# Two attentions whose probabilities are divided before they are turned, with the values stationary and two heads in the column halves

## What is computed

```python
# attention A (one block of 256 keys, so plain causal attention), dh = 64
y_a = softmax(causal(q_a @ k_a.T / 8)) @ v_a
# attention B, q and k of 96 features (64 + 32 rotated), values of 64
y_b = softmax(causal(q_b @ k_b.T / sqrt(96))) @ v_b
merged = sigmoid(gate_a) * (y_a @ w_branch_a) + sigmoid(gate_b) * (y_b @ w_branch_b)
x = x + merged @ w_out
```

## Time and profile before

| | |
|---|---|
| time, 3 runs | 1725.09 us median (1724.26 to 1725.42) |
| the profiled execution | 1723.3 us, span 1721.6 us |
| TensorE busy | 1689.4 us, 98% of the span |
| DVE, ACT, POOL busy | 939.0, 986.0 and 1025.6 us |
| mean granted TensorE clock | 0.997 of full |
| the loop of 16 units | about 86.9 to 141.6 us of the span |
| 84 to 142 us | TensorE busy 56.90 of 58.00 us, DVE 20.51, ACT 36.09, POOL 27.85 |

### The profile page before, as it was taken

One profiled execution on the slowest core, in us unless ns is written; L12 is line 12 of the kernel. 1 busy time (PEld: TensorE's weight loads), 2 busy tenths in 40 slices (PEclk: granted clock), 3 DMA queues, 4 the chain that ended last, 5 costly groups with the idle time before them and its releaser, 6 DMA issues.

```text
span 1721.6 us, 30763 instructions
## 1 busy us (share of the span) xinstructions
PE 1689.4 (98%) x9832; PEld 1457.8 (85%) x9832; DVE 939.0 (55%) x1895; ACT 986.0 (57%) x1894; POOL 1025.6 (60%) x549
## 2 busy tenths in 40 slices
PE   9999999999999999999999989999999999899998
PEld 7887998888888888888888888988999877799997
DVE  6233378897999995555555557752111277421112
ACT  5565654445988885544455466526454565554544
POOL 4846768877777772000000078528888886578886
PEclk9999999999999999999999999999999999999999
DMA  6534545555444446565555645115555554355553
GB/s 224 177 99 133 203 157 183 186 176 187 160 160 160 160 160 197 193 195 193 190 193 193 222 142 159 62 50 177 184 190 186 171 181 138 92 184 184 193 184 121
DMA packets 83074, 288.19 MB, mean 167 GB/s; under 512 B 9264, under 2 KB 9264, under 8 KB 82480
## 3 DMA queue, kind: packets, MB, share of 16 engines
q1 hardware_dynamic: 82560, 286.10, 50.8%
q10 hardware_dynamic: 432, 1.05, 0.2%
HBM read 285.01 MB, written 2.10 MB: 167 GB/s over the span
## 4 chain that ended last, share of the span: by engine, by line
PE 91%; DVE 3%; ACT 3%; POOL 2%; issue 1%; DMA 0%; DVEq 0%; ACTq 0%; POOLq 0%
PE col L943 14%; PE acc L640 14%; PE acc L641 14%; PE acc L642 14%; PE col L945 7%; PE col L677 5%; PE col L679 5%; PE col L678 5%; POOL w_lo L2012 1%; PE mb L958 1%; PE mb L959 1%; PE acc L1155 1%; PE mb L712 1%; ACT hT L1463 1%; ACT w_hi L1439 1%
## 5 line engine op out<-in xcount | busy, mean ns | idle before, releaser
L2012 POOL TENSOR_TENSOR w_lo<-w_raw,w_hi 128x1024 fp32r<-128x1024 f32 (+1 forms) x403 | 954.9, 2387 | 295.9 <-ACT w_hi L1439 295.0
L1439 ACT ACTIVATE w_hi<-w_raw 128x1024 fp32r<-128x1024 f32 (+1 forms) x539 | 564.1, 1050 | 334.9 <-PE acc L642 278.0
L943 PE MATMUL col<-hT,w_hi 128*128 128x512 f32 x1024 | 368.9, 403 | 0.6 <-DVE acc L2527 0.6
L945 PE MATMUL col<-hT,w_lo 128*128 128x256 f32 x1024 | 286.5, 280 | 0.0
L943 PEld LDWEIGHTS col<-hT,w_hi 128*128 128x128 f32 x1024 | 192.3, 188 | 45.8 <-issue 1.5
L640 PE MATMUL acc<-w_hi,W_hi 128*128 128x512 f32 x512 | 199.3, 389 | 0.3 <-DVE act_e L2654 0.3
L642 PE MATMUL acc<-w_hi,W_lo 128*128 128x512 f32 x512 | 199.2, 389 | 0.0
L641 PE MATMUL acc<-w_lo,W_hi 128*128 128x512 f32 x512 | 199.2, 389 | 0.0
L945 PEld LDWEIGHTS col<-hT,w_lo 128*128 128x128 f32 x1024 | 193.5, 189 | 0.0
L2054 POOL TENSOR_SCALAR_AFFINE_SELECT WST<-WST 128x512 f32<-128x512 f32 x1 | 0.9, 940 | 319.5 <-DMA WST<-in_gmlp_w 319.5
L2938 DVE CAST H_hi<-mb 128x256 fp32r<-128x256 f32 x64 | 27.2, 425 | 289.3 <-ACT mb L1865 289.3
(11 more groups left out here) (581 smaller groups left out, 3242.4 us busy)
## 6 DMA issues: line engine op xcount, KB each, us to landing
w_raw<-in_expert_u SPq DMA_DIRECT2D x128, 512.0 KB, 3.2
w_raw<-in_expert_v SPq DMA_DIRECT2D x128, 512.0 KB, 4.3
w_raw<-in_w_mlp SPq DMA_DIRECT2D x128, 512.0 KB, 3.3
w_raw<-in_w_in SPq DMA_DIRECT2D x24, 512.0 KB, 3.8
w_raw<-in_w_qkv_o SPq DMA_DIRECT2D x24, 512.0 KB, 4.2
w_raw<-in_w_query SPq DMA_DIRECT2D x16, 512.0 KB, 3.4
w_raw<-in_w_gate SPq DMA_DIRECT2D x16, 512.0 KB, 3.3
w_raw<-in_w_qkv_e SPq DMA_DIRECT2D x12, 512.0 KB, 3.8
```

The lines of the kernel that those rows point to most:

```text
L943: mm(both, wh[:, k, :], hT[:, :, k, :], start=k == 0, stop=k == KD - 1, skip_group_check=True)
L945: m = mm(both[:, 0, :], wl[:, k, :], hT_hi[:, k, :], start=False, stop=k == KD - 1, skip_group_check=True)
L1439: f(w_hi[:, s, 0:w], w_raw[:, s, 0:w], ACT.Copy).then_inc(sem(f"hi{s}"), 1)
L2012: g.tensor_tensor(w_lo[:, s, 0:w], w_raw[:, s, 0:w], w_hi[:, s, 0:w].bitcast(F32), ALU.subtract).then_inc(sem(f"lo{s}"), 1)
```

## The change

It changes four things in the loop of 16 units and what follows it.

- **Divide first.** DVE gets `normed(u)`: a reciprocal of the two sums of u, then two in-place products on `Pr`, 128 x 128 and 128 x 256, both of them operands in SBUF. It stands at the head of DVE's turn u + 1, before `masked(u + 1)`. TensorE waits for `probs` instead of `exp` before it turns u.
- **Values stationary.** `pair_values(p)` takes the place of `head_values` of two heads: the values (128 x 64) are stationary, the turned probabilities move (256 and 128 columns), the even head's output goes to partitions 0 to 63 and the odd one's to 64 to 127 of `acc[b]`, by feature. It runs at even turns.
- **No turning of the output.** All four `y_map` calls and both `branch_out` calls go. ACT and DVE write the high and low parts straight from `acc[b]` (`heads_hi`, `heads_lo`): A's halves at ACT turns 5 and 9 and DVE turns 8 and 12, B's first half at ACT turn 13, the rest behind the loop.
- **Scores of attention A in pairs**, at even turns, their instructions interleaved.

`bank_free` lets the first chunk of branch A wait bank by bank. Memory is moved to fit: `yA_hi` and `yA_lo` take the place of `Y`.

```diff
-            def scores(u):
+            def scores(*units):
+                for u in units:
+                    if u >= 2:
+                        pe.wait_ge(sem("masked"), u - 1)
+                    if u >= A_H and u % 2 == 0:
+                        pe.wait_ge(sem("qb_E"), upto("qb_E", u - A_H + 2))
+                for u in units:
+                    q, k = qk_of(u)
+                    mm(col[u % 2][:, 0:P], q[:, 0:P], k[:, 0:P], start=True, stop=True)
+                for u in units:
+                    q, k = qk_of(u)
+                    mm(col[u % 2][:, P:3 * P], q[:, P:2 * P], k, start=True, stop=True).then_inc(
+                        sem("scores"), 1)
...
-            def head_values(u):
+            def pair_values(p):
+                b, kk = p % 4 // 2, p % 2
+                pe.wait_ge(sem("pT_E"), upto("pT_E", 2 * p + 2))
+                if p == 0:
+                    pe.wait_ge(sem("ev_kvup"), upto("ev_kvup", 2))
+                if p >= 4 and kk == 0:
+                    pe.wait_ge(sem("yA_E"), b + 1)
+                for kt in range(NT):
+                    for hh in range(2):
+                        h = 2 * p % 8 + hh
+                        v = VC[:, kt, h * 64:(h + 1) * 64] if p < 4 else VB[:, kt, h, :]
+                        o = acc[b][64 * hh:64 * hh + 64, kk * SEQ + kt * P:(kk + 1) * SEQ]
+                        pt = PT[:, hh, 0:2 * P] if kt == 0 else PT[:, hh, 2 * P:3 * P]
+                        m = mm(o, v, pt, start=kt == 0, stop=kt == 1, skip_group_check=True)
+                m.then_inc(sem("pv"), 1)
...
             for u in range(A_H + B_H):
-                pe.wait_ge(sem("exp"), u + 1)
+                pe.wait_ge(sem("probs"), u + 1)
                 if 5 <= u <= 12:
                     pe.wait_ge(sem("qb_E"), upto("qb_E", u - 4))
-                if 13 <= u <= 14:
-                    pe.wait_ge(sem("yA_E"), upto("yA_E", u - 12))
                 causal_fills(u, Pr[:, u % 2, :], "pT", "pT_E")
-                if u + 2 < A_H + B_H:
+                if u + 2 < A_H:
+                    if u % 2 == 0:
+                        scores(u + 2, u + 3)
+                elif u + 2 < A_H + B_H:
                     scores(u + 2)
-                if u:
-                    head_values(u - 1)
+                if u and u % 2 == 0:
+                    pair_values(u // 2 - 1)
                 if 4 <= u <= 11:
+                    pe.wait_ge(sem("pT_E"), upto("pT_E", u))
                     b_map(u)
-                if 12 <= u <= 13:
-                    y_map(0, u - 12, mb[(u + 1) % 2], "yA_T")
                 gate_b(u)
-            head_values(A_H + B_H - 1)
+            pair_values(A_H - 1)
...
# ACT
-                    act.wait_ge(sem(free), upto(free, n - 1))
+                    act.wait_ge(sem(free), n // 2)
+            def heads_hi(m, b, name, pairs):
+                act.wait_ge(sem("pv"), pairs)
+                f(m[:, 2 * b:2 * b + 2, :].rearrange("p k s -> p (k s)"), acc[b][:, :],
+                  ACT.Copy).then_inc(sem(name), 1)
...
+                if u in (5, 9):
+                    heads_hi(yA_hi, (u - 5) // 4, "yA_H", (u - 1) // 2)
+                if u == 13:
+                    heads_hi(yB_hi, 0, "yB_H", 6)
             copy_probs(0, PT, "pT", "pv", A_H + B_H - 1, "pT_E")
             gate_b(1)
+            heads_hi(yB_hi, 1, "yB_H", 8)
             split_to(FIRST["br_a"] + 4)
-            stream_hi("y", range(2))
...
# DVE
+            def normed(u):
+                dve.wait_ge(sem("exp"), u + 1)
+                then(v.reciprocal(sums[:, u, :], sums[:, u, :]))
+                for t, (a, b) in enumerate(((0, P), (P, 3 * P))):
+                    p = Pr[:, u % 2, a:b]
+                    i = v.tensor_scalar(p, p, sums[:, u, t:t + 1], None, ALU.mult)
+                    if t == 0:
+                        go(i)
+                i.then_inc(sem("probs"), 1)
...
             for u in range(A_H + B_H):
+                if u:
+                    normed(u - 1)
                 dve.wait_ge(sem("scores"), u + 1)
...
-                if u == A_H + 2:
-                    branch_out(0)
...
+                if u in (8, 12):
+                    heads_lo(yA_hi, yA_lo, (u - 8) // 4, "yA_H", "yA_E")
+            normed(A_H + B_H - 1)
+            for b in range(2):
+                heads_lo(yB_hi, yB_lo, b, "yB_H", "yB_E")
```

More of the change, by code:

```diff
@@ L633, in row_chunk @@
                         second_half()
-                    if t == 0 and n == 0 and t0_freed:
-                        pe.wait_ge(sem(t0_freed[0]), upto(*t0_freed))
+                    if bank_free:
+                        bank_free(t, n)
                     a, b = splits_of(j)[n]
@@ L809, in b_map @@
                 m.then_inc(sem("qb_T"), 1)
[L811 to L819, removed]
             def gate_b(u):
@@ L842, in gate_b @@
                     m.then_inc(sem(f"used{s}"), 1)
-            scores(0)
-            scores(1)
+            scores(0, 1)
             row_group("kvup", "ev_qup", *from_c(2))
             for u in range(A_H + B_H):
-                pe.wait_ge(sem("exp"), u + 1)
+                pe.wait_ge(sem("probs"), u + 1)
                 if 5 <= u <= 12:
                     pe.wait_ge(sem("qb_E"), upto("qb_E", u - 4))
-                if 13 <= u <= 14:
-                    pe.wait_ge(sem("yA_E"), upto("yA_E", u - 12))
@@ L883, in _, with after_gate_b, of @@
+            def after_gate_b(t, n):
+                if t:
+                    pe.wait_ge(sem("ev_gb"), upto("ev_gb", 3 + n))
+                else:
+                    pe.wait_ge(sem("yB_E"), n + 1)
+            def of(m):
+                return lambda k: lambda t: m[:, k, t * P:(t + 1) * P]
+            pe.wait_ge(sem("yA_E"), 2)
+            for k in range(4):
+                row_chunk(FIRST["br_a"] + k, 0, of(yA_hi)(k), of(yA_lo)(k), k == 0, k == 3,
                           order=(1, 0) if k == 0 else range(NT),
-                          t0_freed=("y", 4) if k == 0 else None)
@@ L885, in _ @@
-            row_group("br_b", "ev_br_a", stream="y", last_by_half=True)
+                          bank_free=after_gate_b if k == 0 else None)
+            row_group("br_b", "ev_br_a", of(yB_hi), of(yB_lo), last_by_half=True)
             merged = [[(kk * SEQ + t * P, M[:, t, (2 * b + kk) * P:(2 * b + kk + 1) * P])
@@ L2414, in masked, with heads_lo @@
                 i.then_inc(sem(name), 1)
[L2416 to L2425, removed]
+            def normed(u):
[7 more added lines that the diff above has]
+                i.then_inc(sem("probs"), 1)
+            def heads_lo(hi, lo, b, name, done):
+                dve.wait_ge(sem(name), upto(name, b + 1))
+                k = slice(2 * b, 2 * b + 2)
+                v.tensor_tensor(lo[:, k, :].rearrange("p k s -> p (k s)"), acc[b][:, :],
+                                hi[:, k, :].bitcast(F32).rearrange("p k s -> p (k s)"),
+                                ALU.subtract).then_inc(sem(done), 1)
             dve.wait_ge(sem("causal"), 3)
             for u in range(A_H + B_H):
+                if u:
+                    normed(u - 1)
                 dve.wait_ge(sem("scores"), u + 1)
@@ L2451, in _ @@
                         then(v.tensor_copy(heads_, turned_), "qb_E")
[L2452 to L2458, removed]
-            branch_out(1)
-            stream_T("y", range(2))
+                if u in (8, 12):
[3 more added lines that the diff above has]
+                heads_lo(yB_hi, yB_lo, b, "yB_H", "yB_E")
             for t, n, a in banks("br_a"):
```

42 lines of the change are left out of this document (9 added, 33 removed).

## The result

The changed kernel takes 1729.38 us (median of 7 executions, 1729.14 to 1730.55) where the kernel before takes 1724.26 us beside it (7 executions, 1722.56 to 1725.59). The ratio is 1.0033, with a 95% interval of 1.0023 to 1.0043: 5.1 us slower. The forecast was +7.4 us.

The account below looks back on a forecast made before the run. TensorE, 91% of the chain that ended last, was taken to bound the kernel, if other engines deliver in time. 6.6 + 1.0 + 1.6 - 2.6 + 0.8 = +7.4 us gave 1730.7 profiled, 1732.5 median; range 1721 to 1738.

Parts of the forecast that it names:

- to turn 2: Loop start: `normed(2)` held by GpSimd's subtractions, so TensorE begins turn 2 at 99.8 instead of 93.2: +6.6 us.
- turns 2 to 6: Turns 4 and 6 wait behind held `normed(4)` and `normed(6)`: 15.5 us for four turns against 14.5, +1.0.
- turns 6 to 12: Closed loop of two units at 7.7 us, `normed` held by POOL; three rounds 23.1 against 21.5: +1.6.
- turn 12 to branch B: Last turns, last pair, four chunks of branch A and 0.8 of waits: 22.7 against 25.3, -2.6.
- clock: Turn 2 after 6 us of idle TensorE runs at the lower level, 1.2 GHz: +0.8, between 0 and 2.
- rival (a): Value pairs: column halves do not run side by side, 0.66 us more for each of eight pairs, +5.3: 1737.8; chance 0.12.
- The savings booked at 7.7 us: TensorE's gain if nothing else is late: scores 2.6, values 2.7, output transposes 1.7, stall 0.7.
- The stall at turn 9: Before turn 9, DVE runs `branch_out(0)` ahead of the copy that turn waits for: 0.7 us, which goes.
- (b): POOL does not hold `normed`, or nearly always misses it: -3.0, 1722.1; chance 0.17.
- (d): Column halves serial, but no hold of `normed`: +2.3, 1727.4; chance 0.09.
- (c): DVE, ACT and POOL keep ahead of TensorE; the whole 7.7 us is gained, 1717.4; chance 0.12.

Follow-up runs that it names:

- the kernel without a product: Changed kernel with `normed` left out, probabilities never divided by their sums, TensorE waiting for the exponentials: 1715.44 us, 8.0 us under the kernel before.
- the accumulating product: Changed kernel with `normed`'s two products written as `tensor_scalar` with an accumulator output that nothing reads: 1720.18 us, ratio 0.9979 to the kernel before.
- the last combined kernel: Changed kernel with products that write an accumulator, and `masked(u)` ahead of `normed(u - 1)` only while u is under 6: 1718.65 us, ratio 0.9968 to before.
- splits spread: Changed kernel with ACT's three splits of turn 1 spread: one in turn 1, one in turn 2, two in turn 3: 1728.84 us, 5.4 over before.
- the mask first: `masked(u)` ahead of `normed(u - 1)` in the changed kernel: 1724.85 us; with products that also write an accumulator: 1719.54 us.

## Why the prediction was right, point by point

The direction and the mechanism were right, and the size was 2.3 us too large, 1.7 of it in the steps up to the gated sum. The steps, each from one mark to the next:

| step | predicted | measured |
|---|---|---|
| to turn 2 | +6.6 | 98.35 - 93.23 = +5.1 |
| turns 2 to 6 | +1.0 | 16.36 - 14.49 = +1.9 |
| turns 6 to 12 | +1.6 | 22.74 - 21.49 = +1.25 |
| turn 12 to branch B | -2.6 | 22.78 - 25.29 = -2.5 |
| clock | +0.8 | in the second row: about +1.7, an estimate |
| sum | +7.4 | +5.7 |

**The start** is the term that was mis-sized. The walk through the splits held: both products of `normed(2)` are held, the first to the end of the second subtraction and the other to the end of the third. But it began too late. I had the two products of `normed(0)` caught one at a time between six rotations, until 88.0; they took 0.91 us and ended at 87.1. ACT's splits therefore ended at 92.97 and not at 94.1, GpSimd's three subtractions at 98.14 instead of 99.3, and turn 2 followed. The alternative that I had kept, that the second product slips in directly, did not happen: that product took 2.45 us.

**Turns 2 to 6.** Turn 4 was forecast at 106.9 and came at 106.73; turn 6 at 115.3 and came at 114.71. The places were right by luck: turn 2 came 1.45 us early, and its lower clock, told of below, took that back. Without it the stretch would have been some 0.2 us over before and not 1.0, by that estimate.

**The rounds** were forecast at 7.7 us and took 7.58 (the pair of values is 0.15 cheaper than in the sum); the 6.56 us that TensorE alone would need are the rounds of the kernel without a product (103.31 to 109.87 to 116.42). The wait for the map copies behind a held `normed` is there: the chain shows 0.82 to 0.84 us of it as "issue" before turns 8, 10 and 12, less than the 1 us that I had named, and 1.25 before turn 6. That these are the copies VectorE's timeline shows, here before turn 6 at 114.71: the products meet the subtraction that GpSimd runs from 110.72 to 113.11, and mask and copy stand behind them.

```profile
112.30 1.16 DVE L2423 TENSOR_SCALAR Pr<-Pr,sums 128x128 f32<-128x128 f32 x2
113.37 0.28 DVE L2413 CUSTOM_DVE_ANT_0 Sm<-col,causal 128x128 f32<-128x128 f32 x1
...
113.93 0.68 DVE L2460 COPY QTB<-mb 96x512 f32<-96x512 f32 x1
```

**TensorE's products.** The pair of values was put at 0.96 us and takes 0.81: no gap appeared where the tile shape changes. By the trace rival (a) is out: in the same column half a pair takes 1.45, in two halves 0.81. Its price, 5.3 us, was near the 5.1 to 6.1 that the serial halves cost. The estimate from the Trainium skill (TensorE: Matmul & The Clock Gate, Measured speedup vs the span model), 1.6 times and 1.13 us, was also too careful; measured is 1.8 times. The savings booked at 7.7 us are 9.3 in the loop of the kernel without products (9.44 less 0.15 from before it). The terms give it: scores 3.1 instead of 2.6, values 10.4 - 8 x 0.81 = 3.9 instead of 2.7, and 1.7 + 0.7 as booked.

**The stall at turn 9** was read too simply. The timeline of before:

```profile
113.90 1.38 ACT L1543 ACTIVATE GB<-acc,rstd 128x512 f32<-128x512 f32 x2 [1.92 <-PE acc L837]
...
116.52 1.42 DVE L2422 TENSOR_TENSOR Y<-acc,sums 128x512 f32<-128x512 f32 x2
...
117.76 0.50 ACT L1553 ACTIVATE Pr<-Sm,mx 128x256 f32<-128x256 f32 x1
...
117.97 0.69 DVE L2449 TENSOR_SCALAR QTB<-mb 96x512 f32<-96x512 f32 x1
```

The exponentials of 9, late because ScalarE reads gate B out first, end at 118.35; the copy behind `branch_out(0)` ends at 118.66, and turn 9 begins at 118.75. Without `branch_out` turn 9 would have begun at about 118.4: only the last 0.3 to 0.4 of the 0.77 us hang on it alone. The kernel without a product has no wait at turn 9; the one with the accumulating product takes 7.19 us for turns 8 and 9 and 6.63 and 6.64 for its neighbours.

**The clock.** After the 5.16 us without work, the granted clock of stretches of 4 us (PE, PEld, DVE, ACT and POOL busy, then the clock) is 0.50 over 99 to 103 us, the lower level, 1.2 GHz:

```profile
95.00:99.00 4.00, 0.65 (x3) 0.50 (x3) 3.85 (x6) 0.12 (x1) 3.14 (x2) 0.85 0.77 235
99.00:103.00 4.00, 4.00 (x20) 2.36 (x19) 1.36 (x7) 1.45 (x6) 0.00 (x0) 0.50 0.51 147
103.00:107.00 4.00, 3.98 (x17) 2.90 (x16) 2.21 (x6) 2.22 (x6) 2.40 (x1) 0.79 0.00 0
```

By the timeline turn 2 takes 104.82 - 98.35 = 6.5 us, where the last combined kernel, with the clock at 1.00, took 97.13 - 93.50 = 3.6 for it: 2.8 us, against 0.8 booked. It reached turn 4 by a path that I had not seen, ScalarE's queue:

```profile
102.42 0.49 ACT L1530 ACTIVATE PT<-mb 128x384 f32<-128x384 f32 x1 [2.55 <-PE acc L804]
102.80 1.05 ACT L1435 ACTIVATE w_hi<-w_raw 128x1024 fp32r<-128x1024 f32 x1
```

The split waits behind a copy that waits for turn 2's pair of values, and the subtraction that holds `normed(4)` until 106.68 waits for the split. The pair ended 102.31 - 98.35 = 3.96 us into turn 2, at the full clock 95.73 - 93.50 = 2.23. So I estimate that about 1.7 us of the late turn 4 is the clock; no run of the changed kernel with the full clock shows it. In the profiled execution of the accumulating product alone, the slowest of its 11, the clock fell too. TensorE had waited 1.70 us there, and then:

```profile
95.00:99.00 4.00, 3.90 (x21) 2.29 (x20) 1.75 (x11) 1.33 (x5) 3.06 (x2) 0.57 0.81 237
```

Its turn 2 took 100.14 - 94.78 = 5.4 us, 1.7 too many.

**The rivals.** (b), no hold, named 1722.1; the kernel without a hold runs at 1720.18, 3.3 under its own before, where the rival had 3.0. Its steps came true nearly one by one: turn 2 at 94.78 (94.7 named), rounds of 6.63, 7.19 and 6.64 us (6.6, 7.2 and 6.6), from turn 12 to branch B 2.9 us less than before (2.6); turns 2 to 6 took 14.8 instead of 13.7, with the lower clock in turn 2. (d), halves serial and no hold, falls with the halves. (c), everything hidden, is what the kernel without products shows. Its 7.7 us is near the 8.0 measured. The condition that I gave for it, `probs(2)` by 93.8, is the one that the changed kernel misses by 4.5 us.

## What to carry to other kernels

When work moves onto VectorE with its operands in SBUF, its duration in the free case says little. Lay every instruction of it over GpSimd's timeline, and count what is queued behind it. Here 0.55 us became up to 4.22, and a form that is slower by itself (0.35 + 0.47 us) made the kernel 8.4 us faster. When you move the work of the engine that holds, look where it lands: here it held another product. And take a change apart: its paired scores alone gain 3.4 us, as much as the whole of it with a product that isn't held (3.3); with the mask first as well it is 5 to 6.

## What the runs showed of the hardware that I had not expected

- Two products of 64 output rows each in the two column halves take 0.81 us against 1.45 in one, eight matmuls each way; no loss showed at the change of tile shape (a pair of scores, in the two row halves, takes 0.85).
- An idle stretch of 1.70 us ahead of turn 2 was followed by a granted clock of 0.57 over 95 to 99 us in one kernel, while in another (splits spread) 2.86 us were followed by 1.00 over the same stretch. What decides between them stays open.
- The product of two SBUF tensors is held like the one with a scalar (4.41 us for a pair against 4.22) and takes 0.63 us for a pair when free, against 0.55.
